# A hybrid decoder trunk with a mixture of experts: the routing done tile by tile inside the attention, and the gate table behind the first expert block

## What is computed

```python
x = x + jnp.concatenate([a, c, s], axis=-1) @ w_out[l]
h2 = rms_norm(x, ln2_g[l]).reshape(B * L, D)
x = x + hierarchical_moe(h2, ...)
return rms_norm(x, final_g)

def hierarchical_moe(h, gw, gb, ew, eb, w_gate, w_up, w_down):
    g_logits = h @ gw + gb                       # 4 groups
    g_p = softmax(g_logits) at g_idx = argmax(g_logits)
    e_logits = (h @ ew + eb) of the 8 experts of that group
    top_v, top_i = lax.top_k(e_logits, 2)
    gate = g_p * softmax(top_v)
    # tokens sorted by expert, padded to blocks; per block:
    act = silu(xb @ w_gate[e]) * (xb @ w_up[e])
    y = (act @ w_down[e]) * gate, added to the token's row
```

## Time and profile before

| | us |
|---|---|
| median of 3 runs (lowest, highest) | 1256.23 (1255.85, 1259.46) |
| profiled execution: time / span of its instructions | 1254.45 / 1252.4 |
| TensorE busy, share of the span | 1144.0, 91% |
| VectorE / ScalarE / GpSimd busy | 472.2 / 360.1 / 290.3 |
| mean granted clock of TensorE, share of full speed | 0.96 |
| DMA traffic | 262 MB, 209 GB/s on average |

### The profile page before, as it was taken

The page is one execution under the profiler, slowest core; times in us unless marked ns, Lnnn a source line. Parts: engine busy times, 40 slices in busy tenths (PEclk is TensorE's granted clock), DMA queues, the critical chain, the costliest instruction groups (busy, mean ns, idle before and its releaser), DMA issues.

```text
span 1252.4 us, 16187 instructions
## 1 busy us (share of the span) xinstructions
PE 1144.0 (91%) x5013; PEld 549.1 (44%) x5014; DVE 472.2 (38%) x1001; ACT 360.1 (29%) x731; POOL 290.3 (23%) x227
## 2 busy tenths in 40 slices
PE   5999999998899999983599999987999999999990
PEld 4898444454355666643233333322333333333330
DVE  3360029942456566317432332322223223323313
ACT  3121100015455555410122222221222222232223
POOL 1010199920000000100212222222121222222223
PEclk9999999999899999995799999988999999999995
DMA  7316211012412111185394699999979999999317
GB/s 247 28 33 134 42 34 34 0 68 72 168 34 68 51 51 52 51 318 235 117 391 127 237 373 384 409 407 413 355 282 381 389 413 372 403 393 380 127 21 271
DMA packets 97323, 261.95 MB, mean 209 GB/s; under 512 B 43180, under 2 KB 60252, under 8 KB 72684
## 3 DMA queue, kind: packets, MB, share of 16 engines
q1 hardware_dynamic: 68868, 243.43, 50.6%
q0 software_dynamic: 11520, 16.81, 6.1%
q10 hardware_dynamic: 16872, 0.92, 0.9%
HBM read 244.86 MB, written 26.74 MB: 217 GB/s over the span
## 4 chain that ended last, share of the span: by engine, by line
PE 85%; DMA 5%; DVE 4%; ACT 2%; ACTq 1%; SPq 1%; issue 1%; POOL 0%; DVEq 0%; POOLq 0%
PE psum L1288 27%; PE psum L1307 13%; PE psum L1021 13%; PE psum L1203 9%; PE psum L1018 3%; PE psum L1161 3%; DMA W<-in_w_gate 3%; PE psum L1276 3%; PE psum L1181 2%; PE psum L1016 2%; PE psum L1295 2%; PE psum L1172 2%; DMA W<-in_x 1%; PE psum L1226 1%; ACTq L756 1%
## 5 line engine op out<-in xcount | busy, mean ns | idle before, releaser
L1288 PE MATMUL psum<-W,RD 128*64 x800 | 371.6, 608 | 14.5 <-DVE RD L1774 14.5
L1289 PE MATMUL psum<-W,RD 128*64 128x512 f32 x800 | 371.6, 608 | 0.0
L1288 PEld LDWEIGHTS psum<-W,RD 128*64 128x64 f32 x800 | 107.3, 140 | 228.1 <-issue 222.2
L1307 PE MATMUL psum<-W,RD 128*64 x400 | 184.0, 603 | 2.6 <-ACT RD L944 2.6
L692 POOL DMA_INDIRECT x_rows<-RD,tabi x49 | 80.2, 1638 | 449.8 <-ACT RD L951 440.1
L1308 PE MATMUL psum<-RD 128*64 128x512 f32 x400 | 184.0, 603 | 0.0
L1755 DVE TENSOR_TENSOR RD<-psum,RD 128x256 f32<-128x256 f32 x50 | 21.3, 425 | 417.7 <-ACT RD L940 417.7
L1021 PE MATMUL psum<-W 128*128 128x512 f32 x384 | 166.4, 593 | 0.6 <-ACT W L774 0.6
L1203 PE MATMUL psum<-W,RD 128*128 128x512 f32 x256 | 119.6, 601 | 5.2 <-DVE W L1575 4.1
L1021 PEld LDWEIGHTS psum<-W 128*128 128x128 f32 x384 | 72.5, 190 | 89.7 <-issue 88.7
L1289 PEld LDWEIGHTS psum<-W,RD 128*64 128x64 f32 x800 | 107.3, 140 | 0.0
(11 more groups left out here) (313 smaller groups left out, 1267.9 us busy)
## 6 DMA issues: line engine op xcount, KB each, us to landing
W<-in_w_up SPq DMA_DIRECT2D x32, 2048.0 KB, 13.3
W<-in_w_gate SPq DMA_DIRECT2D x32, 2048.0 KB, 18.2
W<-in_w_down SPq DMA_DIRECT2D x32, 2048.0 KB, 20.2
W<-in_x SPq DMA_DIRECT2D x16, 512.0 KB, 5.4
W<-in_w_in SPq DMA_DIRECT2D x5, 1024.0 KB, 11.3
W<-in_w_in SPq DMA_DIRECT2D x16, 256.0 KB, 4.3
x_rows<-W SPq DMA_DIRECT2D x8, 512.0 KB, 2.9
h_rows<-RD SPq DMA_DIRECT2D x8, 512.0 KB, 3.9
```

Of the source, the lines that this page charges most:

```text
L1288: pe.matmul(bank(2)[0:HALF].rearrange("p (g n) -> p g n", g=2), x, near, start=k == 0, stop=k == KD - 1)
L1289: ins = pe.matmul(bank(2)[HALF:P], x, upgate1[:, k].rearrange("p g n -> p (g n)"), start=k == 0, stop=k == KD - 1)
L1307: pe.matmul(out[0:HALF], a, W[:, bass.ds(base + (2 * KD * FF + D * k), 512)], start=k == 0, stop=k == FK - 1)
```

## The change

1. **Routing per tile.** The logits are made from the transposed x2 itself, not from the scaled rows; VectorE multiplies them by the tile's root afterwards (`pick_group`). The transposes move from off 14 and 15 to 11 and 13, the logits from 17 to 14. VectorE picks the group at off 15, the experts one step later at off 16, both behind the step's statistics, and at off 19 the place of each pick in its expert (`my_rank`), from products that TensorE makes ahead of the next tile's logits. `macc` carries the counts of all earlier tiles. SI is the slot table, already multiplied by the token number.
2. **Behind the last tile** stay its own picks and places, the block of each expert, the block table and 16 products of 68 columns. The expert of a block is computed with the blocks along the partitions and turned by four small products. `ids_ok` releases the gathers ahead of `idx_ok`.
3. **Gates behind block 0.** Block 0's slot and wait counts are constants, so it needs no table. VectorE computes the gates and multiplies SI by them after its block 0 work; TensorE makes the gate table (16 products of 68 columns) behind block 0's up and gate products; VectorE copies it and only then goes on to block 1.
4. **Places and loads.** x2 has two buffers instead of three, x for the addition moves to slot 0's gate weights, SI lies in slot 2's down weights. So the gate load of slot 0 stands behind the last tile's stores, and the down load of slot 2 behind the gate products.

```diff
@@ SyncE
             load_up(0)
-            load_gate(0)
...
+            load_gate(0)
             load_up(2)
             load_gate(2)
-            for s in range(3):
-                sp.wait_ge(x2_out[s], 16 * ((NT - 1 - s) // 3 + 1))
+            for s in range(2):
+                sp.wait_ge(x2_out[s], 16 * NT // 2)
+            sp.wait_ge(gate_ps, 1)
             load_down(2)
@@ GpSimd
-            pool.wait_ge(tab_ps, 1)
             pool.wait_ge(h2_out, 16 * NT)
...
-            pool.wait_ge(idx_ok, 1)
+            pool.wait_ge(ids_ok, 1)
             for b in range(AHEAD):
                 gather(b)
+            pool.wait_ge(idx_ok, 1)
@@ ScalarE
             def tables(b):
+                if isinstance(b, int) and b == 0:
+                    return 0, [16] * SLOTS
...
+            step(0, 0)
             act.wait_ge(idx_ok, 1)
-            for b in range(4):
+            act.wait_ge(tabg_ok, 1)
+            for b in range(1, 4):
                 step(b // 2, b % 2)
@@ TensorE
                 for b in range(2):
-                    i = tile_at(k, 14 + b)
+                    i = tile_at(k, 11 + 2 * b)
                     if i is not None:
-                        h2_turn(i, b)
-                i = tile_at(k, 17)
+                        x2_turn(i, b)
+                i = tile_at(k, 14)
                 if i is not None:
+                    pe.wait_ge(h2T_ok, i + 1)
+                    if i:
+                        rank(i - 1, bank(5)[:, 64:96]).then_inc(rank_ps, 1)
                     logits(i)
...
             for r in range(16):
                 if r % 8 == 0:
-                    pe.wait_ge(tab_ok, r // 8 + 1)
-                ins = pe.matmul(bank(2)[:, 0:2 * NBLK], slot1h[:, r, :], bval[:, r].rearrange("p n v -> p (n v)"),
-                                start=r == 0, stop=r == 15)
+                    pe.wait_ge(blk_ok, r // 8 + 1)
+                ins = pe.matmul(bank(2)[:, 0:NBLK], SI[:, r, :], blk1h[:, r, :], start=r == 0, stop=r == 15)
...
+            xT(0, 16)
+            step(0, 0)
+            pe.wait_ge(sg_ok, 1)
+            for r in range(16):
+                ins = pe.matmul(bank(3)[:, 0:NBLK], SI[:, r, :], blk1h[:, r, :], start=r == 0, stop=r == 15)
+            ins.then_inc(gate_ps, 1)
             pe.wait_ge(idx_ok, 1)
-            xT(0, 16)
-            for b in range(4):
+            for b in range(1, 4):
                 step(0, b)
@@ VectorE
+            def pick_group(i):
+                dve.wait_ge(lg_ps, i + 1)
+                lg = logit[:, i, :]
+                dve.scalar_tensor_tensor(lg[:, 0:36], bank(5)[:, 0:36], rstd2[:, i:i + 1], rbias[:, :], ALU.mult, ALU.add).then_inc(lg_ok, 1)
...
+            def my_rank(i, src):
+                dve.wait_ge(rank_ps, i + 1)
+                dve.tensor_tensor(MP, MM[:, i], bc(src.unsqueeze(1), [P, 2, EXPERTS]), ALU.mult).then_inc(rank_ok, 1)
+                dve.wait_ge(rank_ok, i + 1)
+                link(dve.tensor_reduce(rsel, MP, AX.X, ALU.add))
...
+                i = tile_at(k, 15)
+                if i is not None:
+                    pick_group(i)
+                i = tile_at(k, 16)
+                if i is not None:
+                    pick_experts(i)
+                i = tile_at(k, 19)
+                if i is not None:
+                    my_rank(i, bank(5)[:, 64:96])
...
             step(0, 0)
+            dve.wait_ge(ge_ok, 1)
+            dve.tensor_reduce(gsum, gdif[:, :, :], AX.X, ALU.add)
...
+            dve.scalar_tensor_tensor(SI, SI, 0.0, bc(gate.rearrange("p t r -> p (t r)").unsqueeze(2), [P, 16, P]), ALU.is_lt, ALU.mult).then_inc(sg_ok, 1)
+            dve.wait_ge(gate_ps, 1)
+            dve.tensor_copy(tabg, bank(3)[:, 0:NBLK]).then_inc(tabg_ok, 1)
+            dve.wait_ge(idx_ok, 1)
             step(0, 1)
```

More of the change, by code:

```diff
@@ L236, in build @@
[L236 to L246, removed]
@@ L251, in build, with late @@
+        d0 = 5120
+        def late(n):
+            nonlocal d0
+            d0 += n
+            assert d0 <= 5376
+            return RD[:, d0 - n:d0]
+        nb, bend, bs, ones, nn, below = late(32), late(32), late(32), late(32), late(6), late(32)
+        col = late(10)
+        stp = late(16)
+        gsum, den, gate = late(8), late(8), late(16).rearrange("p (t r) -> p t r", t=NT)
+        both = RD[:, 5700:5700 + 2 * NBLK].rearrange("p (n b) -> p n b", n=2)
         ident = sb("ident", [P, P])
@@ L422, in build @@
         ex_ye = sem("ex_ye")
-        x2_out = [sem(f"x2_out{i}") for i in range(3)]
+        x2_out = [sem(f"x2_out{i}") for i in range(2)]
         tail_y = sem("tail_y")
@@ L1227, in logits, with rank @@
                 ins.then_inc(lg_ps, 1)
+            def rank(i, out):
+                pe.wait_ge(mm_ok, i + 1)
+                if i == 0:
+                    pe.wait_ge(const_ok, 3)
+                ins = pe.matmul(out, tri[:, :], mbf[:, i, :], start=True, stop=i == 0)
+                if i:
+                    ins = pe.matmul(out, onesb[:, :], macc[:, i, :], start=False, stop=True)
+                return ins
             for k in range(ITERS):
@@ L1585, in _ @@
+            for k in range(ITERS):
+                if k == 6:
+                    dve.memset(logit, -3e38)
+                    dve.wait_ge(const_ok, 4)
+                    for r in range(2):
+                        ins = dve.tensor_scalar(tokv[:, :, r], tokf[:, :], 2.0, 2.0 * L * r - 4.0 * L, ALU.mult, ALU.add)
+                    link(ins)
                 for half in range(2):
@@ L1636, in _ @@
-            edif, eexp = rrv("edif"), rrv("eexp")
-            gate = rrv("gate").rearrange("p (r t) -> p r t", r=2)
-            idx = rrv("idx").rearrange("p (r t) -> p r t", r=2)
-            row, stp, slot, tokv = (rrv(x, 16) for x in ("row", "stp", "slot", "tokv"))
-            link(dve.memset(g8, -3e38))
-            link(dve.tensor_copy(g8[:, :, 0:4], logit[:, :, 0:4]))
-            for i in range(NT):
-                ins = dve.max(mx8[:, i, :], g8[:, i, :])
-            link(ins)
-            for i in range(NT):
-                ins = dve.max_index(gi8[:, i, :], mx8[:, i, :], g8[:, i, :])
@@ new lines, in _ @@
+            link(dve.tensor_scalar(below, bend, tokf[:, 0:1], None, ALU.is_le))
+            pos, third = col[:, 4:5], col[:, 5:6]
+            link(dve.tensor_reduce(pos, below, AX.X, ALU.add))
+            link(dve.tensor_scalar(pos, pos, float(EXPERTS - 1), None, ALU.min))
+            dve.tensor_scalar(third, pos, 1.0, 1.0 / SLOTS, ALU.subtract, ALU.mult)
+            dve.tensor_scalar(col[:, 2:3], pos, 1.0, 1.0 / SLOTS, ALU.add, ALU.mult)
+            link(dve.tensor_scalar(col[:, 3:4], pos, 1.0 / SLOTS, None, ALU.mult))
```

297 lines of the change are left out of this document (146 added, 151 removed).

## The result

| | before | changed |
|---|---|---|
| median, us (20 runs each) | 1255.34 | 1258.48 |
| lowest, highest | 1251.52, 1259.46 | 1256.18, 1260.31 |
| profiled execution: time / span | 1254.45 / 1252.4 | 1259.16 / 1257.4 |

The ratio is 1.0027, with a 95% interval of 1.0018 to 1.0035. The kernel became 3 us slower. I had predicted 1248.7, with a range of 1244 to 1255.5; the result lies outside of it, on the other side of no change, though just within the 0.3% that I had called no change.

The account below looks back on a forecast made before the run. TensorE, busy 91% of the span, was taken to wait for a serial routing chain on VectorE. Terms +1.5 - 1.6 - 14.0 + 6.6 = -7.5 us gave 1248.7 us from the median of 1256.23, range 1244 to 1255.5.

Parts of the forecast that it names:

- Term 1: Attention: VectorE's added pick and place instructions make TensorE wait some 0.3 us in four heavy steps, +1.5 us in all.
- The second insert: Attention, the step after the heavy one: the expert pick, 8 instructions, some 1.6 us, costed at nothing.
- My bound of 6: Upper bound of the attention cost in us: pause and margin missing half the time, 1.5 us a step.
- rival B: VectorE's small steps in attention and chain: 0.32 us each in place of 0.21 costs 10 us, result 1258.7; 10%.
- my sign for this term: Attention: TensorE idle above 2 us in 400 to 520 would show the attention term wrong.
- Term 2: Last tile's logits: less work after the last addition saves 2.8 us, its later start costs 1.2; -1.6 us.
- Term 3: Chain from last logits to index table: 15.2 us against 29.2, so -14.0 us.
- the upper bound, 7.2: Chain's table products: 4.95 us expected, bounds 3.4 and 7.2 us.
- Term 4: Seam from block 0's products to block 1's first: 9.5 us in place of 2.9, so +6.6 us.
- Rival A: Expert blocks: ScalarE waits for slot 2's late down weights; result 1253.6 to 1260 for 13.3 to 20.2 us loads; 15%.
- Rival C: Expert stage: the weight stream does not start earlier, TensorE waits longer further on, time stays near 1256; 9%.

Follow-up runs that it names:

- e2: Changed kernel, with the rest of the group pick and place moved later in the last attention step with scores only; 1255.59 us, ratio 0.9999 to the kernel before.
- e5: Changed kernel, with all picks, places and rank products moved behind the last logits, only the operation on the logits left in attention; 1281.9 us (one run).
- e9: Changed kernel plus eight more dependent 8-column VectorE operations in the heavy step's insert, tiles 0 to 5; 1273.38 us, ratio 1.0149 to the kernel before.
- e1: Changed kernel, with VectorE preparing block 1 before it waits for the gate products and copies the gate table; 1253.69 us, ratio 0.9983 to the kernel before.
- e8: Changed kernel with e1, e3, the seventh tile's places earlier and idle TensorE products (2, 3, 5, 5); 1240.46 us, ratio 0.9870 to the kernel before.
- e10: e8 with the third slot's down weights loaded once the slot table is scaled, before the gate products end; 1238.87 us, ratio 0.9873 to the kernel before.
- e4: Changed kernel plus unread TensorE products (4, 8, 9) where it waits in the routing chain; 1259.08 us, ratio 1.0027 to the kernel before.
- e11: Kernel before the change plus idle TensorE products only (1, 8, 8, 11); 1252.30 us, ratio 0.9970 to the kernel before.
- e3: Changed kernel, with picks and places spread to the ends of later steps in every tile; 1255.27 us, ratio 0.9996 to the kernel before.

## Why the prediction was wrong, step by step

**Term 1, attention: predicted +1.5, measured +7.8** (9.25 at its end, less the 1.43 that stood at step 10). The step that failed is "The insert exceeds the pause by 1.05 us, the margin behind it is 0.75, so TensorE waits some 0.3 us, in four steps of that kind". Three things in it were off. The insert takes 3.6 us (516.60 to 520.17), not 3.1, as L1665 is two writes of 128 columns in 0.60. The pause was read once, at 416, and taken for all four steps: three of them cost 0.7 to 1.0 us, not 0.3, and step 31 has no scores behind it; it cost 3.3 (e2 and e5). And a TensorE that idles does not lose only the idle time: the clock fell there, and 1.8 of the 3.3 us are its part. A second thing that I had put at nothing was not: the moved transposes and the missing buffer, 1.5 us in e5, whose cause stays open. The small products and their steps cost another 0.5. The second insert did cost nothing. My bound of 6 did not hold. The price of a small step, 0.21, was right (0.20 in e9), so rival B as I had put it (0.32 a step) is false, and that its 1258.7 is near the measured time is luck. Its sign and its place were right: steps in attention are paid in full from the insert's present length on. And my sign for this term, TensorE idle above 2 us in 400 to 520, did not show (1.64 us): the largest loss came behind 520.

**Term 2, last logits: predicted -1.6, measured -0.64** from the end of attention. The picks ahead of the last half of x2 are on the path: in e9 two doses of 1.6 us in the drain cost 4.4. That the products ran at half clock (3.50 us) is no difference, they had before (3.63).

**Term 3, the chain: predicted 15.2 us, measured 18.6 (29.2 before).** The small and wide steps up to the table products took 10.7 us; my figures were 6.9 + 0.45 + 2.15 = 9.5. The table products took 7.1 in place of 4.95: "Three microseconds at the slow rate and the rest at the fast one" was the mis-sized part. I had read the clock's return from products of 136 columns; with 68 it did not return at all, and the upper bound, 7.2, was the value. The rule of the Trainium skill on small operations (VectorE: DVE Perf Modes, The TRN2 errata) holds by the rows, 0.20 us for 8 columns where 512 take 0.69, yet was no loss in the chain: it became 10.7 us shorter.

**Term 4, the seam: predicted 9.5 us, measured 9.56.** Each piece stands in the trace: transposes, 32 passes in 3.54, the copy at 621.06, the reads of 2.55, then 626.38. e1 shows that none of what is behind the gate products had to be there.

**From the indices to the first product I kept 6.3 us; it was 7.4,** as the gather took 5.4 us.

**Rival A** did not cost anything in the changed kernel: the load issued at 621.12 had landed by 628.87, in 7.75 us, near the 7.5 of the fastest up load in the earlier trace rows; ScalarE's first copy waited 11.6 us for it, and the seam hid that. It showed when the seam was gone (e8, e10). **Rival C** is false; the waits for w_gate are the same.

So against the sum the profile lost 6.3 us more in attention, 1.0 in term 2, 3.3 in the chain and 1.0 at the gather, had 1.4 already at step 10, and gained 0.5 in block 0: -7.5 became +5.1. At the end of the profiled run 4.7 are left, 3.3 without the 1.4 of step 10, and the medians show 3.1. I had named the case: "The prediction fails if the seam passes 13 us or attention ends over 5 us later." The mistake in the chances was to give everything slower than 1255.5 to one price, that of a small step, when an insert could just as well meet a step without slack.

## What to carry to other kernels

Work is hidden only if the slack is there at each place it goes to; read it at the last repetition too, where the next step has less ahead of what waits. An engine that is made to wait for a late by-product should first do what others wait for. And where TensorE must idle ahead of many products, idle work sized to just under the pause (here 0.89 us a product) can be worth more than the rebuilt chain: 10.9 us on top of a change that alone lost 3; sized over the pause, as in e4, it gives nothing.

## What was not expected of the hardware

Halving the width of the table saved little: 32 passes of 136 columns take 4.24 us at 2.4 GHz (two rows of 2.12 in e11), of 68 columns 3.69. The clock weighs far more, 7.09 us at 1.2 GHz. The profiles also differ ahead of anything that was changed, by up to 2.6 us at step 3 (e3, with a granted clock of 0.96 over 0 to 80 us where the kernel before had 1.00; but e9 has 0.96 too and is 1.15 late), and again in step 8, where the same eight products take 4.08 us in e2 and 5.67 in e1. Behind step 10 that variation is gone: up to step 30 the changed kernel and e2, the same program so far, keep a distance of 0.73 to 0.77 us. So a difference of two traces should be taken from the last instruction that both share.
